# Pair steps of a stick-breaking attention layer: the scores of two units move from the even slots to the odd slots, between projection and values

## The chip, the cores and the metric

The kernel runs on one core of a Trainium2 chip. The metric is the device time of one execution, in microseconds. Before the change the median of three executions is 1330.95 us (1330.93 to 1331.21).

## What is computed

One decoder layer on 1024 tokens of width 1024, all in float32: RMS norm, an input projection, stick-breaking attention with 16 heads of 64 columns, cross-attention of 4 heads to 256 memory tokens, an output projection, and a SwiGLU block. The part that the change touches is the stick-breaking attention:

```
q, k, v, xq = split_cols(h @ w_in, [D_MODEL, D_MODEL, D_MODEL, X_WIDTH])
def block(args):                      # 128 queries of every head
    z = jnp.einsum('bhqd,bhkd->bhqk', qi, k).astype(jnp.float32) * SCALE
    past = kpos[None, :] < tpos[:, None]
    log_fail = jnp.where(past, jax.nn.log_sigmoid(-z), 0.0)
    after = lax.cumsum(log_fail, axis=3, reverse=True) - log_fail
    a = jnp.where(past, jnp.exp(jax.nn.log_sigmoid(z) + after), 0.0)
    return jnp.einsum('bhqk,bhkd->bhqd', a.astype(v.dtype), v)
```

The kernel takes sigmoid(-z) ("fail") and sigmoid(z) ("succ"), builds the running product of fail from right to left, and multiplies it with succ: that is the weight a.

## The kernel before

Five engines run five hand-written programs and meet through counting semaphores: TensorE (PE), VectorE (DVE), ScalarE (ACT), GpSimd (POOL) and the DMA queue of SyncE (SP). An engine works its program in the written order, so the order of the code is the order of the work.

**Precision.** Every matrix product with float32 operands is made of three matmuls: each operand is split into a high part (written by ACT, names with `_h`) and a low remainder (written by DVE, names with `_l`). A "chunk" below is the three matmuls of 512 columns that one block of 128 input rows adds to a projection.

**Pair steps.** The 16 heads are taken as 8 pairs. A pair step `s` (`pe_step`, `act_step`, `dve_step`) computes the attention of pair `s` and, woven into it, the q, k and v projections of pair `s + 1`: six parts of 512 tokens, eight chunks each (`pe_part`), which share one PSUM bank, `j_ps[:, 0]`. A part may begin only when ACT (`act_evac_half`, L494) and, for q and k, DVE (`dve_evac_half`, L601) have taken the previous part out of that bank. The steps 0 to 6 are of this kind (in a loop but for the outer ones); in the last step, 7, there is no next pair, and the first tiles of the output projection (`pe_project`, L1182) stand in the place of the parts.

**Units and slots.** The causal triangle of a pair is cut into ten units, 0 to 9 (`UNITS`), of 384 to 512 key columns for both heads. A step has ten slots. The work of unit `u` goes round the engines:

- PE makes its scores (`pe_scores`, L409) into one of two PSUM areas, `z2[u % 2]`, by parity of the unit. It waits for the second sigmoid of unit `u - 2`, which read the same area.
- ACT takes two sigmoids: `act_fail` (L506), which waits for the weights of unit `u - 2`, and `act_succ` (L512), which waits for the turns of unit `u - 2`.
- DVE scans fail for both heads (`dve_scan`, L617 and L622) and multiplies (`dve_weights`, L630).
- PE turns the weights, 6 or 8 transposes into `t_ps` (`pe_transposes`, L418), in slot `u`. It waits for the weights, and for the low part of the previous unit's turns, since `t_ps` is one buffer.
- ACT writes the high part of the turns, `a_h` (`act_high`, L521), DVE the low part, `a_l` (`dve_low`, L647).
- PE multiplies with v (`pe_values`, L436, 8 or 16 matmuls), after slots 1, 2, 3, 5, 7 and 9 (`VALUES_AT`). It waits for `a_l` of the last unit of its group and, in a group that opens a new bank content, for ACT's copies of the earlier result (`act_low_rows`, L533 and L534, four per group; `ROWS_AT` puts them in slots 2, 3 and 6).

After slot 9 `pe_v` (L391) turns the next pair's v; ACT and DVE take that out of `t_ps` too (L499, L606) before the turns of the next unit 0 may start. In slot `u` DVE's program has: scans of unit `u + 1` (with the low part of a projection half between the two heads, after `EVAC_LOW`), low part of unit `u`, weights of unit `u + 1`. The change leaves DVE's, POOL's and SP's programs as they are.

In an even slot PE has turns, then the scores of units `u + 2` and `u + 3`, then chunks, then perhaps values. In an odd slot it has turns, chunks, values. ACT has in each slot `u`: high part of `u`, copies of rows, fail and succ of unit `u + 2`, then a weight conversion (L487) or the high part of a finished projection half.

Of the kernel before, what the change touches and what calls it, by code (L numbers as in the profile page):

```python
# [19 lines left out]
def trunk(nc, x, mem, norms, w_mem_kv, w_out, w_gate, w_up, w_down, sb_w_in, out):  # L20
# [25 lines left out]
    NU = len(UNITS)  # L46
# [5 lines left out]
    ROWS_AT = {2: 0, 3: 2, 6: 5}  # L52
    SCANS_TO = (4, 6, 8, 12, 14, 16, 18, 20, 22, 24)
    CARRY_BY = {4: 4, 5: 4, 8: 7, 9: 8}
    PARTS = {1: (0, 5, 8), 2: (1, 0, 8), 3: (2, 0, 8), 4: (3, 0, 4), 5: (3, 4, 8), 6: (4, 0, 4), 7: (4, 4, 8),
             8: (5, 0, 4), 9: (5, 4, 8)}
    PART_END = {1: 0, 2: 1, 3: 2, 5: 3, 7: 4, 9: 5}
    EVAC_LOW = {2: 0, 3: 1, 4: 2, 6: 3}
    M0 = 2
# [28 lines left out]
    with ExitStack() as ctx:  # L88
# [354 lines left out]
        def pe_step(pe, s, par, last=False):  # L443
            for u in range(NU):
                if u:
                    pe_transposes(pe, s, u)
                if u == 0 and isinstance(s, int) and s == 0:
                    pe_scores(pe, s, 2, par)
                    pe_part(pe, s + 1, 1 - par, 0, 0, 2)
                    pe_scores(pe, s, 3, par)  # L450
                    pe_part(pe, s + 1, 1 - par, 0, 2, 3)
                    pe_transposes(pe, s, u)
                    pe_part(pe, s + 1, 1 - par, 0, 3, 5)
                    continue
                if u % 2 == 0:
                    for ahead in (u + 2, u + 3):
                        if ahead < NU:
                            pe_scores(pe, s, ahead, par)
                        elif not last:
                            pe_scores(pe, s + 1, ahead - NU, 1 - par)  # L460
                if not last and u == 0:
                    pe_part(pe, s + 1, 1 - par, 0, 0, 2)
                    pe_transposes(pe, s, u)
                    pe_part(pe, s + 1, 1 - par, 0, 2, 5)
                elif not last:
                    pe_part(pe, s + 1, 1 - par, *PARTS[u])
                else:
                    if u == 0:
                        for i, some in AHEAD:
                            pe_project(pe, i, some=some)  # L470
                        pe_transposes(pe, s, u)
                    for i, some in FILL.get(u, ()):
                        pe_project(pe, i, some=some)
                if u in VALUES_AT:
                    pe_values(pe, s, VALUES_AT[u], par)
            if not last:
                pe_v(pe, s + 1, 1 - par, 1 + TUSE * s + NU)
# [65 lines left out]
        def act_step(act, s, par, last=False):  # L543
            side = iter(SPLITS) if last else None
            for u in range(NU):
                if last and u - 1 in FILLED:
                    act_part(act, FILLED[u - 1])
                if u == 0:
                    act_fail(act, s, 2)
                    if last:  # L550
                        act_low_rows(act, s - 1, NU - 1, heads=(0,))
                act_high(act, s, u)
                if isinstance(s, int) and s == PAIRS - 2:
                    for i in PRE_AT.get(u, ()):
                        act_split(act, i)
                if last:
                    for _ in range(SPLIT_AHEAD[u]):
                        act_split(act, next(side))
                if u in ROWS_AT:
                    act_low_rows(act, s, ROWS_AT[u])  # L560
                nxt = (s, u + 2) if u + 2 < NU else (s + 1, u + 2 - NU) if not last else None
                if nxt:
                    if u:
                        act_fail(act, *nxt)
                    act_succ(act, *nxt)
                if last:
                    if u == 0:
                        act_low_rows(act, s - 1, NU - 1, heads=(1,))
                    for _ in range(SPLIT_RATE[u] - SPLIT_AHEAD[u]):
                        act_split(act, next(side))  # L570
                    continue
                for k in CONV_AT.get(u, ()):
                    if k < 6 or not (isinstance(s, int) and s == PAIRS - 2):
                        act_w(act, s + 1 + k // 6, k % 6, (1 - par + k // 6) % 2)
                if u in PART_END:
                    act.wait_ge(s_pj, W0 + 6 * (s + 1) + PART_END[u] + 1)
                    act_evac_half(act, s + 1, PART_END[u], 1 - par)
# [221 lines left out]
        for i in PRE + SPLITS + LATER + SECOND:  # L799
# [5 lines left out]
        SPLIT_AHEAD = (0, 0, 0, 0, 0, 0, 0, 0, 1, 1)  # L805
        DVE_RATE = (0, 0, 1, 1, 1, 1, 1, 2, 2, 2)
        DVE_AHEAD = (0,) * NU
        LOWER, UPPER = (0, 1), (2, 3, 4, 5)
        AHEAD = [(0, (0, 1))]
        FILL = {0: [(0, (2, 3, 4, 5))], 1: [(1, (0, 1, 2, 3))], 2: [(1, (4, 5))], 3: [(2, None)], 4: [(3, LOWER)],  # L810
                5: [(3, UPPER)], 6: [(4, None)], 7: [(5, None)], 8: [(6, None)], 9: [(7, None)]}
        FILLED = {0: 0, 2: 1, 3: 2, 5: 3, 6: 4, 7: 5, 8: 6, 9: 7}
        assert sum(SPLIT_RATE) == len(SPLITS) and sum(DVE_RATE) + sum(DVE_AHEAD) == sum(LOW[i][0] for i in SPLITS)
# [381 lines left out]
        def act_part(act, i):  # L1195
            act.wait_ge(s_op, i + 1)
            act.activation(part[:, i], out_bank(i), ACT.Copy).then_inc(s_pt, 1)
# [1063 lines left out]
        def _(pe):  # L2261
# [66 lines left out]
            for s in range(2):  # L2328
                pe_step(pe, s, s)
# [42 lines left out]
```

## Time and profile before

| | |
|---|---|
| median of three executions | 1330.95 us |
| the profiled execution | 1331.02 us |
| its span, first to last instruction | 1329.2 us |
| PE busy | 1314.0 us, 99% of the span |
| DVE busy | 1030.5 us, 78% |
| ACT busy | 680.7 us, 51% |
| POOL busy | 419.6 us, 32% |
| DMA queues, mean | 54 GB/s |
| granted TensorE clock | 1.0 in the whole span |

The profile page gives busy shares for the whole program; the stretch that the change touches is the part from 119 to 606 us, where the pair steps run. In the rows of the trace the first number is the start in us from the beginning of the span and the second the time from there to the end of the last instruction in the row. The matmuls overlap in the pipeline, so a matmul of 512 columns lasts 0.39 us in the records, while the next one starts 0.23 us after it. Start to start is the cost that counts.

### The profile page before, as it was taken

Reading aid. Unit: us, or ns where it says so; the run is one execution under the profiler, and the core shown is the slowest. Engines: PE = TensorE matmul, PEld = TensorE weight load, DVE = VectorE, ACT = ScalarE, POOL = GpSimd, SP = SyncE. Lnnn points to the kernel's source line nnn. Section 1 sums busy time; section 2 is a strip of 40 time slices with the busy share of each in tenths; the row PEclk is TensorE's granted clock in tenths of the full one; section 3 lists DMA queues with packets and bytes.
Section 4 is the critical chain, followed back from the end, with each engine's and each line's share of the span. In section 5 each row is a group of like instructions: output and inputs, shape, how many; then the busy total and the mean of one; then the engine's idle time right before and its main releaser. Section 6 shows DMA issues by size and latency. Waiting matters only on the chain.

```text
span 1329.2 us, 20179 instructions
## 1 busy us (share of the span) xinstructions
PE 1314.0 (99%) x6854; PEld 1088.7 (82%) x6854; DVE 1030.5 (78%) x1153; ACT 680.7 (51%) x1154; POOL 419.6 (32%) x307
## 2 busy tenths in 40 slices
PE   7999999999999999999999999999999999999999
PEld 5887888888888888888888788888888888888887
DVE  6577898887978899995258877878778787777866
ACT  7577676666666677773254433343343433333340
POOL 2000000000000001214034764747546484664721
PEclk9999999999999999999999999999999999999999
DMA  7100100010010101206111222121212112122103
GB/s 254 32 25 24 33 25 25 25 33 25 24 32 24 32 24 40 104 9 199 31 40 32 73 74 61 40 72 32 71 47 63 61 36 69 39 71 62 42 32 127
DMA packets 91484, 71.87 MB, mean 54 GB/s; under 512 B 4256, under 2 KB 75936, under 8 KB 91424
## 3 DMA queue, kind: packets, MB, share of 16 engines
q1 hardware_dynamic: 91424, 71.07, 17.0%
q8 instruction: 37, 0.61, 0.2%
q14 instruction: 23, 0.19, 0.0%
HBM read 65.03 MB, written 4.19 MB: 52 GB/s over the span
## 4 chain that ended last, share of the span: by engine, by line
PE 93%; DVE 2%; ACT 2%; POOL 1%; issue 1%; DMA 0%; ACTq 0%; POOLq 0%; DVEq 0%
PE ps L1476 27%; PE ps L378 16%; PE ps L1651 14%; PE ps L1182 8%; PE ps L436 5%; PE ps L418 5%; PE ps L409 4%; PE ps L1261 3%; PE ps L344 3%; PE ps L1706 2%; PE ps L958 1%; PE ps L898 1%; ACT junk L839 1%; PE ps L1069 1%; PE ps L1134 1%
## 5 line engine op out<-in xcount | busy, mean ns | idle before, releaser
L1661 DVE TENSOR_TENSOR x<-ps,x 128x2048 f32<-128x2048 f32 x70 | 160.3, 2290 | 92.6 <-PE ps L1651 92.6
L655 POOL TENSOR_TENSOR o_t<-o_t,pv_low 128x256 f32 x24 | 21.4, 890 | 445.1 <-ACT o_t L534 445.1
L1444 DVE TENSOR_TENSOR part_l<-part_x,part_h 128x512 fp32r<-128x512 f32 x140 | 141.7, 1036 | 25.3 <-POOL part_x L1422 17.9
L1639 POOL TENSOR_TENSOR bl<-bx_B,bh 128x512 fp32r<-128x512 f32 x70 | 93.2, 1331 | 208.8 <-ACT bh L1635 208.8
L378 PE MATMUL ps<-hh,w_h 128*128 128x512 f32 x336 | 139.1, 414 | 0.0
L521 ACT ACTIVATE a_h<-ps 128x1024 fp32r<-128x1024 f32 (+1 forms) x80 | 75.4, 942 | 116.0 <-PE ps L418 115.7
L378 PE MATMUL ps<-hh,w_l 128*128 128x512 f32 x336 | 131.6, 392 | 0.0
L378 PE MATMUL ps<-hl,w_h 128*128 128x512 f32 x336 | 131.0, 390 | 0.0
L1476 PE MATMUL ps<-ft_h,part_h 128*128 128x512 f32 x320 | 124.5, 389 | 0.0
L1476 PE MATMUL ps<-ft_l,part_h 128*128 128x512 f32 x320 | 124.5, 389 | 0.0
L1476 PE MATMUL ps<-ft_h,part_l 128*128 128x512 f32 x320 | 124.5, 389 | 0.0
L1487 ACT ACTIVATE kept<-ps 128x512 f32<-128x512 f32 x60 | 35.7, 595 | 158.2 <-PE ps L1476 158.2
L1651 PE MATMUL ps<-bh,ah 128*128 128x512 f32 x280 | 109.1, 390 | 0.9 <-DVE x L1661 0.6
L1651 PE MATMUL ps<-bl,ah 128*128 128x512 f32 x280 | 108.9, 389 | 0.0
L617 DVE TENSOR_TENSOR_SCAN fail<-fail,own 128x257 f32<-128x257 f32 (+3 forms) x128 | 101.1, 828 | 9.4 <-ACT fail L506 9.4
L647 DVE TENSOR_TENSOR a_l<-ps,a_h 128x1024 fp32r<-128x1024 f32 (+1 forms) x80 | 89.0, 1113 | 22.5 <-ACT a_h L521 22.2
L1635 ACT ACTIVATE bh<-bx_B 128x512 fp32r<-128x512 f32 x70 | 44.2, 631 | 102.5 <-PE ps L1651 97.9
L1476 PE MATMUL ps<-f_h,part_h 128*128 128x512 f32 x240 | 93.4, 389 | 0.0
L1476 PE MATMUL ps<-f_l,part_h 128*128 128x512 f32 x240 | 93.4, 389 | 0.0
L1476 PE MATMUL ps<-f_h,part_l 128*128 128x512 f32 x240 | 93.4, 389 | 0.0
L1437 ACT ACTIVATE part_h<-part_x 128x512 fp32r<-128x512 f32 x140 | 82.9, 621 | 19.6 <-POOL part_x L1411 14.7
L630 DVE TENSOR_TENSOR succ<-fail,succ 128x1024 f32<-128x1024 f32 (+2 forms) x80 | 91.0, 1137 | 0.7
(290 smaller groups left out, 3390.6 us busy)
## 6 DMA issues: line engine op xcount, KB each, us to landing
w_raw<-in_sb_w_in SPq DMA_DIRECT2D x52, 256.0 KB, 2.8
bx_B<-in_w_down SPq DMA_DIRECT2D x44, 256.0 KB, 3.0
part_x<-in_w_gate SPq DMA_DIRECT2D x40, 256.0 KB, 2.9
part_x<-in_w_up SPq DMA_DIRECT2D x40, 256.0 KB, 2.8
wo_raw<-in_w_out SPq DMA_DIRECT2D x20, 256.0 KB, 3.3
x_in<-in_x SPq DMA_DIRECT2D x8, 512.0 KB, 7.5
x<-in_x SPq DMA_DIRECT2D x16, 256.0 KB, 5.4
out<-x SPq DMA_DIRECT2D x16, 256.0 KB, 2.0
```

The costliest lines, as they stand in the source:

```text
L378: mm = pe.matmul(j_ps[:, 0], w[:, kc // 4, kc % 4], h[:, kc, half * BANK:(half + 1) * BANK], start=(kc == 0 and i == 0), stop=(kc == KC - ...
L521: act.activation(home(a_h), t_ps[:, :, 0:len(blocks_of(u)) * P].rearrange("p h (j q) -> p h j q", q=P), ACT.Copy).then_inc(s_th, 1)
L617: dve.tensor_tensor_scan(back, back, own[:, BANK - w:BANK + 1][:, ::-1], 0.0, ALU.mult, ALU.max).then_inc(s_scan, 1)
L630: done = dve.tensor_tensor(g, f[:, :, 1:w + 1], g, ALU.mult)
L647: dve.tensor_tensor(home(a_l), t_ps[:, :, 0:len(blocks_of(u)) * P].rearrange("p h (j q) -> p h j q", q=P), home(a_h).bitcast(F32), ALU.sub ...
L1182: mm = pe.matmul(out_bank(i), o[:, t % 4 * P:t % 4 * P + P], w[k][:, :], start=(at_ == 0 and j == 0), stop=(at_ == len(order) - 1 and j == 2))
L1437: act.activation(part_h[p][:, :, :].rearrange(flat), part_x[m][p][:, :, :].rearrange(flat), ACT.Copy).then_inc(s_fh, 1)
L1444: dve.tensor_tensor(part_l[m][p][:, :, :].rearrange(flat), part_x[m][p][:, :, :].rearrange(flat), part_h[p][:, :, :].rearrange(flat).bitca ...
L1476: mm = pe.matmul(product_bank(m, p), w[:, k], g[:, k], start=(p in (0, 1, 3) and k == 0 and i == 0), stop=(k == 3 and i == 2), skip_group_ ...
L1639: pool.tensor_tensor(bl[(par + k) % 2][:, :], bx[B_OPS[k]][:, :], bh[(par + k) % 2][:, :].bitcast(F32), ALU.subtract).then_inc(s_bw, 1)
L1651: mm = pe.matmul(ps[:, t], g[:, t * P:(t + 1) * P], w[:, :], start=(k in (0, 4, 5) and i == 0), stop=(i == 2), skip_group_check=True)
L1661: dve.tensor_tensor(o, ps[:, 0:4], o, ALU.add).then_inc(s_x2, 1)
```

## The change

PE: the scores of two units leave the even slots. They now stand in the odd slots, behind the chunks and in front of the values, and are those of units `u + 3` and `u + 4`. The chunks are split anew: slots 4, 6 and 8 have six chunks each and slots 5, 7 and 9 two (before, four in each); slot 0 has seven chunks of the first part and slot 1 one (before, five and three). The last step's output projection is divided in the same manner (`LOWER`, `UPPER`, `AHEAD`, `FILL`).

ACT: in the odd slots fail and succ of unit `u + 2` go ahead of the high part of unit `u`. In the even slots the order stays.

```diff
-    PARTS = {1: (0, 5, 8), 2: (1, 0, 8), 3: (2, 0, 8), 4: (3, 0, 4), 5: (3, 4, 8), 6: (4, 0, 4), 7: (4, 4, 8),
-             8: (5, 0, 4), 9: (5, 4, 8)}
+    PARTS = {1: (0, 7, 8), 2: (1, 0, 8), 3: (2, 0, 8), 4: (3, 0, 6), 5: (3, 6, 8), 6: (4, 0, 6), 7: (4, 6, 8),
+             8: (5, 0, 6), 9: (5, 6, 8)}
...
                     pe_transposes(pe, s, u)
-                    pe_part(pe, s + 1, 1 - par, 0, 3, 5)
-                    continue
-                if u % 2 == 0:
-                    for ahead in (u + 2, u + 3):
-                        if ahead < NU:
-                            pe_scores(pe, s, ahead, par)
-                        elif not last:
-                            pe_scores(pe, s + 1, ahead - NU, 1 - par)
-                if not last and u == 0:
-                    pe_part(pe, s + 1, 1 - par, 0, 0, 2)
+                    pe_part(pe, s + 1, 1 - par, 0, 3, 7)
+                elif not last and u == 0:
+                    pe_part(pe, s + 1, 1 - par, 0, 0, 4)
                     pe_transposes(pe, s, u)
-                    pe_part(pe, s + 1, 1 - par, 0, 2, 5)
+                    pe_part(pe, s + 1, 1 - par, 0, 4, 7)
...
+                if u % 2:
+                    for ahead in (u + 3, u + 4):
+                        if ahead < NU:
+                            pe_scores(pe, s, ahead, par)
+                        elif not last:
+                            pe_scores(pe, s + 1, ahead - NU, 1 - par)
                 if u in VALUES_AT:
                     pe_values(pe, s, VALUES_AT[u], par)
...
+                nxt = (s, u + 2) if u + 2 < NU else (s + 1, u + 2 - NU) if not last else None
+                if nxt and u % 2:
+                    act_fail(act, *nxt)
+                    act_succ(act, *nxt)
                 act_high(act, s, u)
...
-                nxt = (s, u + 2) if u + 2 < NU else (s + 1, u + 2 - NU) if not last else None
-                if nxt:
+                if nxt and u % 2 == 0:
                     if u:
                         act_fail(act, *nxt)
                     act_succ(act, *nxt)
...
-        LOWER, UPPER = (0, 1), (2, 3, 4, 5)
-        AHEAD = [(0, (0, 1))]
-        FILL = {0: [(0, (2, 3, 4, 5))], 1: [(1, (0, 1, 2, 3))], 2: [(1, (4, 5))], 3: [(2, None)], 4: [(3, LOWER)],
+        LOWER, UPPER = (0, 1, 2, 3), (4, 5)
+        AHEAD = [(0, (0, 1, 2))]
+        FILL = {0: [(0, (3, 4, 5))], 1: [(1, (0, 1, 2, 3))], 2: [(1, (4, 5))], 3: [(2, None)], 4: [(3, LOWER)],
```

PE's program at the boundary of slots 5 and 6 of an ordinary step, before: values of slot 5, turns of unit 6, scores of units 8 and 9, then the first of four chunks (the numbers behind names only tell buffers apart).

```order
L378 MATMUL ps<-hh,w_l_77 128x512
L436 MATMUL ps<-a_h,v_s_71 128x256
...
L418 MATMUL ps<-ident,succ 128x128 x6
L409 MATMUL ps<-k_h_69,q_h_67 128x512 x2
L409 MATMUL ps<-k_l_70,q_h_67 128x512 x2
L409 MATMUL ps<-k_h_69,q_l_68 128x512 x2
...
L378 MATMUL ps<-hh,w_h_74 128x512
```

The same place now:

```order
L378 MATMUL ps<-hh,w_l_77 128x512
L409 MATMUL ps<-k_h_69,q_h_67 128x512 x2
L409 MATMUL ps<-k_l_70,q_h_67 128x512 x2
L409 MATMUL ps<-k_h_69,q_l_68 128x512 x2
...
L436 MATMUL ps<-a_h,v_s_71 128x256
...
L418 MATMUL ps<-ident,succ 128x128 x6
L378 MATMUL ps<-hh,w_h_74 128x512
```

The scores have gone from behind the turns of unit 6 to ahead of the values of slot 5, and the chunks of slot 6 stand right behind the turns.

ACT's program in slot 5 of an ordinary step, before: the high part of unit 5's turns, then fail and succ of unit 7, then the high part of a finished half of k (the register rows only compute semaphore targets).

```order
L521 ACTIVATE a_h<-ps 128x8x128
L503 REGISTER_ALU
L506 ACTIVATE fail<-ps 128x2x512
L512 ACTIVATE succ<-ps 128x1024
L576 REGISTER_ALU
L494 ACTIVATE k_h_65<-ps 128x512
```

And now:

```order
L505 ACTIVATE fail<-ps 128x2x512
L510 REGISTER_ALU
L511 ACTIVATE succ<-ps 128x1024
L520 ACTIVATE a_h<-ps 128x8x128
L578 REGISTER_ALU
L493 ACTIVATE k_h_65<-ps 128x512
```

Both sigmoids have moved ahead of the high part. The same holds in slots 1, 3, 7 and 9.

## Rows read from the trace of the kernel before

**Rows 1.** Windows, an ordinary step: length, then PE, PEld, DVE, ACT, POOL busy

```profile
243.76:303.72 59.96, 59.96 (x379) 50.55 (x378) 51.33 (x60) 39.92 (x59) 3.57 (x4) 1.00 0.09 27
```

**Rows 2.** Timeline of PE, slots 7 and 8 of that step

```profile
287.49 1.03 PE L418 MATMUL ps<-ident,succ 128*128 128x128 f32 x8
288.28 0.48 PE L378 MATMUL ps<-hh,w_h 128*128 128x512 f32 x1
288.60 0.40 PE L378 MATMUL ps<-hl,w_h 128*128 128x512 f32 x1
...
291.10 0.28 PE L436 MATMUL ps<-a_h,v_s 128*128 128x256 f32 x1
...
292.93 1.06 PE L418 MATMUL ps<-ident,succ 128*128 128x128 f32 x8
293.92 0.33 PE L409 MATMUL ps<-k_h,q_h 64*128 64x128 f32 x2
...
295.33 0.50 PE L378 MATMUL ps<-hh,w_h 128*128 128x512 f32 x1
```

**Rows 3.** Timeline of ACT and DVE, slot 7

```profile
288.56 1.03 ACT L521 ACTIVATE a_h<-ps 128x1024 fp32r<-128x1024 f32 x1 [0.95 <-PE ps L418]
289.49 1.02 ACT L506 ACTIVATE fail<-ps 128x1024 f32<-128x1024 f32 x1
290.39 1.03 ACT L512 ACTIVATE succ<-ps 128x1024 f32<-128x1024 f32 x1
...
289.62 1.22 DVE L647 TENSOR_TENSOR a_l<-ps,a_h 128x1024 fp32r<-128x1024 f32 x1 [0.43 <-ACT a_h L521]
290.77 1.22 DVE L630 TENSOR_TENSOR succ<-fail,succ 128x1024 f32<-128x1024 f32 x1
```

**Rows 4.** Timeline, slot 6: turns on PE, both sigmoids on ACT

```profile
282.29 0.82 PE L418 MATMUL ps<-ident,succ 128*128 128x128 f32 x6
...
285.67 1.03 ACT L506 ACTIVATE fail<-ps 128x1024 f32<-128x1024 f32 x1
286.60 1.02 ACT L512 ACTIVATE succ<-ps 128x1024 f32<-128x1024 f32 x1
```

**Rows 5.** The chain that ended last: scores of units 8 and 9

```profile
283.10 1.59 PE ps L409 x12
```

**Rows 6.** Timeline of PE, step 0: scores behind a chunk

```profile
124.37 0.39 PE L378 MATMUL ps<-hh,w_l 128*128 128x512 f32 x1
124.69 0.33 PE L409 MATMUL ps<-k_h,q_h 64*128 64x128 f32 x2
```

**Rows 7.** Timeline of PE: values that had waited for DVE, step 6

```profile
542.34 0.39 PE L436 MATMUL ps<-a_h,v_s 128*128 128x256 f32 x1
```

**Rows 8.** Timeline, from the turns of v to unit 1

```profile
243.76 1.03 PE L391 MATMUL ps<-ident,v_t 128*128 128x128 f32 x8
...
249.70 0.93 DVE L647 TENSOR_TENSOR a_l<-ps,a_h 128x768 fp32r<-128x768 f32 x1
...
250.32 0.39 PE L378 MATMUL ps<-hh,w_l 128*128 128x512 f32 x1
250.69 0.88 PE L418 MATMUL ps<-ident,succ 128*128 128x128 f32 x6
```

**Rows 9.** Timeline of DVE, slots 1 and 2

```profile
253.40 0.95 DVE L647 TENSOR_TENSOR a_l<-ps,a_h 128x768 fp32r<-128x768 f32 x1
...
255.19 0.67 DVE L601 TENSOR_TENSOR q_l<-ps,q_h 128x512 fp32r<-128x512 f32 x1
```

**Rows 10.** Timeline of the last step: PE and ACT, slots 2 and 5

```profile
556.48 1.06 PE L418 MATMUL ps<-ident,succ 128*128 128x128 f32 x8
...
559.84 0.38 ACT L534 ACTIVATE om_t<-ps 64x256 f32<-64x256 f32 x1
...
572.98 1.09 PE L418 MATMUL ps<-ident,succ 128*128 128x128 f32 x8 [0.51 <-DVE succ L630]
```

## The prediction, made before the changed kernel ran

> **What bounds the kernel now.** I read the page first: PE is busy in 99% of the span at a granted clock of 1.0. The windows view of one ordinary pair step says the same of the stretch that the change touches: PE's records fill 59.96 of 59.96 us, DVE's 51.33, ACT's 39.92 [rows 1]. So a step lasts as long as PE's instructions take, start to start, and there is nothing to win from a wait that goes away, since hardly one is left. The change can shorten a step only where it makes PE's changes of work cheaper, and lengthen it wherever PE comes to a wait before the other engines are ready. So I read the timelines of PE, ACT and DVE for how long before its need each hand-over is ready.
>
> In slot 7 PE starts the turns at 287.49, the chunks 0.79 later, and the values at 291.10, 3.61 after the turns [rows 2]. The values need unit 7's low part. ACT starts the high part 1.07 after the turns' start, DVE the low part 1.06 after that, and it ends at 290.84, 3.35 after the turns [rows 3]. From the end of a DVE instruction to the start of PE's that waited for it are 0.06 us (249.70 + 0.93 to 250.69) [rows 8]. So the values are free to start at 3.41 and do at 3.61: the reserve is 0.2 us. This round (turns, high part, low part, values) is what the change lengthens.
>
> **The change, part by part.** The amounts are the same: no matmul, sigmoid, scan or DMA is added or removed. All is in the order.
>
> *Changes of work on PE.* Scores use 64 rows of the array for each head, all else 128. Before, a batch of scores stands between turns and chunks: turns to scores cost 0.99 instead of the 0.79 of turns to chunks (0.20), the batch of units 0 and 1 takes 1.41 up to the first chunk, whose record is 0.50 instead of 0.48 (0.02) [rows 2]. Together 1.63. Now it stands between chunks and values. From a chunk's last matmul to scores are 0.32 instead of 0.23 (0.09) [rows 6]. How scores are followed by values the trace does not show. Below, the values' first matmul costs nothing more; above, the 0.11 by which a first values matmul that had waited is longer (0.39 against 0.28) [rows 7, 2]. That gives 1.50 to 1.61 for a batch, so 0.02 to 0.13 saved, five batches a step. I take 0.06, near the upper price, since the first chunk behind scores pays too: 0.3 us a step.
>
> The Trainium skill, "TensorEngine Tiling (Array Packing)", section "Key Properties", says that a change of tiling mode drains TensorE. By that rule alone the saving would be nothing, since each batch has one change in and one out before as well as after, and the step's sum would be 0.3 higher; the rows above show that the two ways in are not priced alike (0.20 and 0.09).
>
> *ACT's order in odd slots, slot 7.* fail of unit `u + 2` can run early: it waits only for the weights of unit `u`, which are ready when the turns start. succ must wait until the turns have read its buffer, so it starts where the high part started, 1.07 after the turns' start. It takes 0.90 (from fail to succ, 289.49 to 290.39) [rows 3]. ACT works in order, so the high part starts at 1.97, the low part at 3.03, ends at 4.25, and the values may start at 4.31. PE has now two chunks there: 0.79, then six matmuls (0.32 for the first, 0.227 for each other by the eleven from 288.60 to 291.10, 1.46), 0.09, scores 1.41: it arrives at 3.75 [rows 2, 6]. That alone is a wait of 0.56.
>
> In slot 7 ACT is late besides. Slot 6 has the four copies of rows; its fail of unit 8 starts 3.38 and its succ 4.31 after the turns of unit 6 [rows 4]. Then fail of unit 9 comes at 5.22 and succ at 6.13. PE has in slot 6 now six turns (0.59, two fewer than 0.79 at 0.10 each) and 18 matmuls (4.18), so the turns of unit 7 start at 4.77, and succ could have gone at 5.84. So everything is 0.29 later: the values wait 0.85.
>
> *Slots 5 and 9.* The same sum. In slot 5 the scores are those of units 8 and 9, 1.59 [rows 5]: PE arrives at 3.93, the wait is 0.38. In slot 9 succ is of 384 columns a head, an estimate of 0.70 from the 0.90 for 512, so the values are free at 4.11; the scores of units 2 and 3 lie between 1.41 and 1.59: 0.18 to 0.36, I take 0.25. In slots 1 and 3 the longer round is hidden: slot 1's values are of unit 0, and in slot 3 eight chunks stand ahead.
>
> *Slot 0.* The turns of unit 1 start 6.93 after the turns of v, when DVE has unit 0's low part [rows 8]. That side (v out, copies of rows, fail and scan of unit 2, low part) stays. PE arrives before at 250.55, so it waits 0.14. Now it has no scores there but seven chunks: 0.79 + 12 matmuls 2.82 + turns 0.59 + 9 matmuls 2.14 = 6.34. Wait 0.59, 0.45 more.
>
> *Slot 2.* The part that starts here needs DVE's low part of the q half before it, which ended 5.17 after the turns of unit 1 (255.86 − 250.69) [rows 8, 9]; DVE's side of it stays. Scores used to stand between turns and that part. Now PE has, from the turns of unit 1: 0.59, one chunk 0.87 (its end to scores included), scores at most 1.59, eight values 0.92 (half of the 1.83 for sixteen) [rows 2] plus 0.11, turns 0.79: 4.87. Ready at 5.23. Wait 0.36. In slot 6 the like wait (low part of k) comes out at nothing or 0.1.
>
> *An ordinary step:* 0.85 + 0.38 + 0.25 + 0.45 + 0.36 = 2.29, less 0.3: about +2.0. DVE and POOL have no instruction moved, and the stretch after the steps is PE's own work, so nothing gives this back. I take steps 0 to 6 as seven such steps: +14.0.
>
> *The last step.* Slot 2 has only six projection matmuls. Its values wait for the copies of rows, which end 3.74 after the turns of unit 2 (560.22 − 556.48) [rows 10]; the scores (1.6) covered that. Now PE arrives at 0.79 + 1.46 = 2.25: wait 1.55. In slot 4, PE waits 0.51 for the weights of unit 5 already [rows 10]; it has six more matmuls (1.37) for the scores that left (1.63): 0.26 more. Slot 5 adds 0.38. Together +2.2; an unpriced one is output tile 4, which comes sooner behind the turns of unit 6 and needs DVE's last split.
>
> **Sum:** 14.0 + 2.2 = 16.2 us on the profiled 1331.02 (its span of 1329.2 and 1.8 around it; 0.07 above the median): 1347.
>
> **The rivals.**
>
> *Only the value waits count,* 1341. The waits of slots 0 and 2 are differences of long sums on both sides, and a small shift of DVE's work could clear them. Left: 0.85 + 0.38 + 0.25 − 0.3 = 1.2, times seven, and about 2 for the last step: +10. Against it: slot 0 had a wait even before. Chance 15%.
>
> *Faster:* PE's cheaper entry into scores counts and no wait shows. Place: the values of slots 5, 7 and 9. It holds if the low part comes before PE: the round would have to be 0.56 shorter than 4.31 in slot 7, for instance if succ did not hold up the high part. Then 40 batches at 0.02 to 0.13 save 1 to 5 us: 1328. For it: PE's share is full now, and every wait that I found is below 1 us. Against it: the round is made of four measured pieces in strict order, its reserve before was 0.2, and the change adds 0.90. Chance 8%.
>
> *No change,* both sides cancel: 1331. Chance 3%.
>
> *The lateness runs on:* 1354. ACT's lateness after slot 6 or DVE's in slots 6 to 8 adds waits at turns too, and the last step's split costs 1 or more: 3 us a step. For it: DVE has 51 of 60 us of work, and low part, weights and scan follow each other. Against it: in even slots six chunks (4.97 with the turns) stand against a round of 4.56 (high part, low part and weights start 1.07, 1.06 and 1.15 apart, the weights take 1.22, and 0.06 [rows 3, 8]). Chance 8%.
>
> *The forecast:* 66%.
>
> **Numbers.** 1347 us. Its own bounds: waits of slots 9 and 2 and the saving at their ends, 1.6 to 2.4 a step, 1343 to 1351. With the first rival below and part of the last above, the range is 1338 to 1352. A measurement of this kernel tells about 0.2% (2.7 us) from no change. Slower by more than that: 66 + 15 + 8 = 89%; within: 3%; faster: 8%.
>
> **What would show it.** An ordinary step (from turns of v to turns of v) should be 62 us for 59.96. PE should have waits named for DVE's low part ahead of the values of slots 5, 7 and 9, near 0.4, 0.85 and 0.25; ahead of the turns of unit 1, 0.6; ahead of the first chunk of slot 2, 0.36, for DVE's q_l; and in the last step one of 1.5 for ACT's copies. The high part in slot 7 should start some 2.2 after the turns. I am wrong if values start with no gap behind scores, or if scores to values cost much more than 0.11: at 0.3 the two values that don't wait (slots 1 and 3) would add 0.4 a step.

## The result, and the profile after

The changed kernel takes 1353.27 us (median of five executions, 1351.8 to 1355.2) against 1330.95 (five executions, 1330.73 to 1331.22); the ratio is 1.0169, 95% interval 1.0158 to 1.018. It is 22.3 us slower. The forecast was 1347, range 1338 to 1352: the sign was right, the time 1.3 us above the range.

The windows view of the changed kernel, the eight pair steps from one turn of v to the next. Columns: stretch, its length, busy us of PE, PEld, DVE, ACT, POOL, then granted clock, DMA share, GB/s.

```profile
120.40:185.88 65.48, 63.39 (x403) 51.95 (x402) 55.52 (x66) 41.38 (x59) 2.78 (x3) 1.00 0.09 25
185.88:247.94 62.06, 60.31 (x378) 50.05 (x377) 51.90 (x60) 39.92 (x59) 3.57 (x4) 1.00 0.09 27
247.94:310.05 62.11, 60.43 (x379) 50.03 (x378) 51.91 (x60) 39.92 (x59) 3.54 (x4) 1.00 0.09 26
310.05:372.14 62.09, 60.41 (x378) 50.03 (x377) 51.81 (x60) 39.92 (x59) 3.55 (x4) 1.00 0.09 27
372.14:438.01 65.87, 62.16 (x378) 51.21 (x377) 51.94 (x60) 39.92 (x59) 3.55 (x4) 0.97 0.09 25
438.01:500.14 62.13, 60.47 (x378) 50.03 (x377) 51.80 (x60) 39.93 (x59) 3.56 (x4) 1.00 0.09 26
500.14:562.80 62.66, 60.68 (x378) 49.98 (x377) 56.77 (x65) 45.64 (x70) 10.65 (x8) 1.00 0.13 40
562.80:626.58 63.78, 58.69 (x343) 47.56 (x342) 52.34 (x57) 41.05 (x63) 7.47 (x7) 1.00 0.18 61
```

The third row answers to [rows 1]: the step has become 2.15 us longer, while PE's busy time is up only by 0.47 and DVE's by 0.58. PE waits now. Before, the same eight stretches were 63.34, 60.03, 59.96, 59.91, 59.95, 59.92, 60.85 and 59.99. The differences are 2.14, 2.03, 2.15, 2.18, 5.92, 2.21, 1.81 and 3.79, together 22.23. That is the whole loss: PE's long run of output projection behind the steps (255 matmuls in the chain, 57.84 us both times) begins at 626.58 for 604.34. So there are three things to explain: a toll of about 2.1 in each of seven steps (14.7), an event of 3.7 in step 4 alone, and the last step's 3.8.

Step 0 and the last step are not like the others in the amount of work. The same view of the kernel before, step 0 and the last step:

```profile
120.10:183.44 63.34, 61.19 (x386) 50.87 (x385) 55.12 (x66) 41.36 (x60) 2.79 (x3) 1.00 0.09 26
544.34:604.33 59.99, 59.43 (x361) 49.45 (x360) 52.05 (x57) 41.43 (x64) 7.21 (x7) 1.00 0.18 63
```

Step 0 still makes the scores of units 2 and 3 at its head and now makes five more batches, one more than before (PE x403 for x386). The last step has one fewer (x343 for x361), since step 6 makes that of its units 2 and 3. A batch is about 1.6 us. So the last step is 3.8 longer with 1.6 less to do, and 1.6 of what step 0 has added is work; it is only 2.14 longer because PE had waited there for the low part twice before, 1.08 and 1.06 in the records.

PE's waits in the changed kernel: who waited for whom, us in total, times, the longest.

```profile
PE ps L436 <- DVE a_l L649: 7.4, 15, 0.7
...
PE ps L418 <- DVE a_l L649: 2.9, 7, 0.5
PE ps L378 <- issue: 2.9, 2, 2.4
...
PE ps L436 <- ACT om_t L533: 1.4, 1, 1.4
PE ps L418 <- DVE v_s L608: 1.4, 1, 1.4
PE ps L1184 <- DVE o_l L999: 0.8, 1, 0.8
PE ps L418 <- DVE succ L632: 0.7, 1, 0.7
...
PE ps L378 <- DVE q_l L603: 0.4, 1, 0.4
```

The reader should see that the page's share (PE 98% busy) hides them: in the steps each is under a microsecond but for three, and the list counts only what is left after the modelled end of the matmul before. Start to start is more exact, and for that I laid the step's PE records side by side. The timeline of the changed kernel in slot 7, all three engines (it answers to [rows 2, 3]):

```profile
292.43 1.03 PE L418 MATMUL ps<-ident,succ 128*128 128x128 f32 x8
292.72 1.03 ACT L505 ACTIVATE fail<-ps 128x1024 f32<-128x1024 f32 x1
...
293.62 1.05 ACT L511 ACTIVATE succ<-ps 128x1024 f32<-128x1024 f32 x1
...
294.53 1.05 ACT L520 ACTIVATE a_h<-ps 128x1024 fp32r<-128x1024 f32 x1
295.62 1.22 DVE L649 TENSOR_TENSOR a_l<-ps,a_h 128x1024 fp32r<-128x1024 f32 x1 [1.20 <-ACT a_h L520]
...
296.97 0.38 PE L436 MATMUL ps<-a_h,v_s 128*128 128x256 f32 x1 [0.72 <-DVE a_l L649]
```

The high part starts 2.10 after the turns (before: 1.07), the low part ends 4.41 after them, and the values start at 4.54 for 3.61.

Step 2 of both kernels in pieces, each from its first start to the first start of the next piece, in us (worked out from PE's timelines; for scores that stood in another slot before, the slot is named):

| piece | before | after | added by waiting |
|---|---|---|---|
| slot 0, the nine matmuls ahead of the turns of unit 1 | 2.30 | 2.71 | 0.41 |
| slot 2, turns to first chunk (where none waits: 0.80) | | 1.16 | 0.36, for q_l |
| slot 5, scores of units 8 and 9 (before in slot 6) | 1.60 | 1.99 | 0.39 |
| slot 7, scores of units 0 and 1 (before in slot 8) | 1.41 | 2.20 | 0.79 |
| slot 9, scores of units 2 and 3 (before in slot 0) | 1.59 | 1.78 | 0.19 |
| sum | | | 2.14 |
| all turns, q_l's wait left out | 8.91 | 8.11 | |
| all chunks, the wait of slot 0 left out | 34.16 | 34.54 | |
| all values | 9.30 | 9.72 | |

The last three rows are the price of the changes of work: 0.80 less, 0.38 more, 0.42 more. The batches cost the same in either place.

Then the event of step 4, which no row of before has. PE's timeline of the changed kernel where step 4 begins:

```profile
372.14 1.03 PE L391 MATMUL ps<-ident,v_t 128*128 128x128 f32 x8
375.60 0.49 PE L378 MATMUL ps<-hh,w_h 128*128 128x512 f32 x1 [2.42 <-issue]
375.93 0.39 PE L378 MATMUL ps<-hl,w_h 128*128 128x512 f32 x1
376.16 0.40 PE L378 MATMUL ps<-hh,w_l 128*128 128x512 f32 x1
376.39 0.60 PE L378 MATMUL ps<-hh,w_h 128*128 128x512 f32 x1
376.79 0.63 PE L378 MATMUL ps<-hl,w_h 128*128 128x512 f32 x1
...
379.77 0.42 PE L378 MATMUL ps<-hh,w_l 128*128 128x512 f32 x1
380.03 0.81 PE L418 MATMUL ps<-ident,succ 128*128 128x128 f32 x6
```

After the turns of v PE does nothing for 2.4 us, and the releaser is "issue": no semaphore held it. Then come three matmuls at the usual pace and eight at 0.40 to 0.43 start to start for 0.23, about half pace. The windows view of those 3.64 us of the changed kernel (the clock is the number ahead of the DMA share):

```profile
376.39:380.03 3.64, 3.64 (x10) 2.78 (x9) 1.23 (x1) 0.51 (x1) 0.38 (x1) 0.53 0.14 42
```

The granted clock is 0.53 here for 1.00 in the ordinary steps: nearly all of this stretch at the lower of the clock's two levels, 1.2 GHz, and ahead of it PE had stood still. The place is where PE's loop over steps 2 to 5 (two steps a turn) branches back to its start. The page's part on DMA queues says how much code was fetched. Before, it was 37 packets of instructions; now:

```profile
q8 instruction: 46, 0.75, 0.2%
```

Nine packets more, of 16 KB each by the row. The DMA view of a stretch alone says when. The changed kernel, 371.9 to 499, which is the second turn of the loop (steps 4 and 5):

```profile
q8 instruction: 8, 0.13, 0.5%
```

In the kernel before the same view from 353 to 483.5 has no packet of instructions at all: its loop ran its second turn on code that was already there. In the changed kernel that code was fetched again. (The ninth packet starts at 371.29, just ahead of the event.)

The last step, the four longest of PE's waits (timeline of the changed kernel, rows apart):

```profile
567.28 0.85 PE L418 MATMUL ps<-ident,succ 128*128 128x128 f32 x6 [1.36 <-DVE v_s L608]
...
580.80 0.36 PE L436 MATMUL ps<-a_h,v_s 128*128 128x256 f32 x1 [1.43 <-ACT om_t L533]
...
595.03 1.09 PE L418 MATMUL ps<-ident,succ 128*128 128x128 f32 x8 [0.72 <-DVE succ L632]
...
606.49 0.50 PE L1184 MATMUL ps<-wo_h,o_h 128*128 128x512 f32 x1 [0.83 <-DVE o_l L999]
```

### The profile page after: what moved, and what is told of

Its sections match the earlier page's. It is cut to its first block, busy times and chain, and to the rows that moved or that the text cites. A ratio compares the mean times of both kernels' runs of the same rounds, so it can differ in the third digit from the quotient of the medians.

```text
span 1351.5 us, 20169 instructions
## 1 busy us (share of the span) xinstructions
PE 1320.2 (98%) x6854; PEld 1086.1 (80%) x6854; DVE 1034.5 (77%) x1153; ACT 680.7 (50%) x1154; POOL 419.7 (31%) x307
## 4 chain that ended last, share of the span: by engine, by line
PE 80%; DVE 6%; ACT 6%; issue 5%; POOL 1%; DMA 0%; ACTq 0%; DVEq 0%; SPq 0%; POOLq 0%
PE ps L1478 27%; PE ps L1653 14%; PE ps L378 11%; PE ps L1184 7%; PE ps L436 5%; PE ps L418 3%; PE ps L1263 3%; PE ps L344 3%; DVE a_l L649 2%; ACT a_h L520 2%; DVE fail L619 2%; PE ps L1708 2%; PE ps L409 1%; ACT fail L505 1%; DVE succ L632 1%
## 5 line engine op out<-in xcount | busy, mean ns | idle before, releaser
L1439 ACT ACTIVATE part_h<-part_x 128x512 fp32r<-128x512 f32 x140 | 83.0, 621 | 19.6 <-POOL part_x L1413 14.7
```

The lines of the kernel that those rows point to most:

```text
L1439: act.activation(part_h[p][:, :, :].rearrange(flat), part_x[m][p][:, :, :].rearrange(flat), ACT.Copy).then_inc(s_fh, 1)
```

## The experiments

### The event: is it the order of the work, or the loop?

**The changed kernel with PE's loop written out.**

```diff
-            with pe.Fori(1, LOOPS) as m:
+            for m in range(1, LOOPS):
```

> The changed kernel with PE's loop over the middle pair steps written out (steps 2 to 5 in line, no branch back); the other engines keep their loops, and the order of the work is the same. In the changed kernel the fifth step lasts 65.87 us and its neighbours 62.1: PE stands 2.42 us for nothing but issue right where its loop has branched back, and then ten matmuls run at half the clock. Theory A (code loading): the loop's code is fetched again when it branches back, so in line there is no such stall: all middle steps 62.1, no fall of the clock, about 3.8 us less than the changed kernel, 1349.5. Rival B (the stall comes with the new order of the work): it stays, 1353. The Trainium skill, Advanced Engine Details and Errata, section ISA Cache, gives TensorE's instruction cache as 128 KB in lines of 16 KB; that is for theory A, and it says nothing on how lines are thrown out.

Measured: 1349.61 us (1349.53 to 1349.73), ratio 1.0140 (1.0123 to 1.0157). Step 4 is 62.08, the half pace is gone, and there are 43 packets. The event is gone with the branch back: 3.7 us. Writing the loop out moves the code too, so this alone doesn't prove that the branch is to blame. The place of the stall does the rest: in each of the four profiles that have it, PE stops right behind the branch back.

**The kernel before, with 72 waits on a semaphore long reached (36 instructions) ahead of the pair steps.**

```diff
+            for _ in range(72):
+                pe.wait_ge(s_id, 1)
```

> The kernel before with 36 more instructions ahead of PE's first matmul (waits that are met while PE is idle anyway), so that its loop over the middle steps starts where the changed kernel's does. Theory A (code loading, decided by where the loop lies in the code): the fifth step gets the stall after the branch back and the half clock, 59.9 to about 63.7, 1334.8 in all, and the instruction queue moves some 46 packets instead of 37. Rival B (the stall comes with the new order): nothing changes, 1331.0, 37 packets. Between them: the loop is refetched but PE's work ahead hides it.

Measured: 1335.01 us (1334.68 to 1335.68), ratio 1.0031 (1.0019 to 1.0044). The order of the work is that of before, but the stall is there in step 4 (63.14 for 59.95), with 46 packets again. That is 3.2 of the 3.7 us by which the span of the profiled execution is longer; the rest was not traced. PE's timeline of this run:

```profile
363.77 1.03 PE L391 MATMUL ps<-ident,v_t 128*128 128x128 f32 x8
367.21 0.50 PE L409 MATMUL ps<-k_h,q_h 64*128 64x512 f32 x2 [2.41 <-issue]
...
370.57 0.50 PE L378 MATMUL ps<-hl,w_h 128*128 128x512 f32 x1 [0.59 <-issue]
```

All six executions lie above 1334. So the stall does not need the moved scores: 36 instructions ahead of the loop are enough. The half pace isn't part of it each time: here none follows.

**The kernel before with its loop written out**, the control (the same edit as the first).

> Control: the kernel before with PE's loop over steps 2 to 5 written out. Theory A: it had no reload (37 instruction packets, no step longer than 60.0 among 1 to 5), so nothing changes but the number of packets, 43: 1331 within 0.5. Rival B: the loop's branch costs the kernel before something too: 1329 or less.

Measured: 1331.87 us (1331.8 to 1331.92, ten executions), ratio 1.0006 (0.9996 to 1.0016), steps of 60.03. Writing the loop out wins nothing where there is no stall; the time is even 0.8 us longer than the 1331.07 measured beside it.

**The changed kernel, 160 such waits (80 instructions), and with 320 (160 instructions).**

> The changed kernel with 80 more instructions that do nothing (waits on a semaphore already reached) in PE's program ahead of the pair steps. Theory A: whether PE's loop is fetched again when it branches back depends on where its start and end lie against the 16 KB packets in which code comes in. The end moves further into its last packet, the start stays in the same one: the stall stays, 46 instruction packets or more, time near 1353 to 1354. Rival B: the stall is chance or hangs on an exact instant: then it comes and goes, 1349.5 or 1353.

> As the run before, with 160 more instructions in place of 80. Theory A: the start of the loop now lies in the next packet, and the loop spans one packet fewer, as in the kernel before: no stall of 2.4 us and no half clock after it, all ordinary steps 62.1, 38 or 39 instruction packets in all, time 1349.5 to 1350. Rival B: any shift keeps it: 1353.

Measured: 1354.15 us (1353.72 to 1354.6) and 1363.05 us (1362.65 to 1363.55). The totals mislead, because the waits themselves were not free this time: step 0 begins at 124.28 and 133.96 for 120.40 (in the run with 36 they were hidden). By the steps, both are without the event. The nearer one's step 4 in the windows view:

```profile
376.00:438.10 62.10, 60.44 (x378) 50.04 (x377) 51.81 (x60) 39.89 (x59) 3.57 (x4) 1.00 0.09 25
```

Both have 38 packets. Less their 3.9 and 13.6 us they stand at 1350.3 and 1349.5. For the far one theory A was right but for the cost of the waits; for the near one it was wrong: I expected the stall to stay. That code ahead of the loop can take the event away as well as bring it is borne out (the four executions of each run lie within 0.9 us); my rule for which places are bad is not.

### The ordinary step: which part of the change costs what?

**The kernel before with ACT's new order alone** (sigmoids ahead of the high part in odd slots; PE's program is that of before).

```diff
+                nxt = (s, u + 2) if u + 2 < NU else (s + 1, u + 2 - NU) if not last else None
+                if nxt and u % 2:
+                    act_fail(act, *nxt)
+                    act_succ(act, *nxt)
                 act_high(act, s, u)
...
-                if nxt:
+                if nxt and u % 2 == 0:
```

> The kernel before with one part of the change alone: in odd slots ACT takes fail and succ of unit u + 2 ahead of the high part of unit u; PE's order is the old one. Theory: the values of slots 5, 7 and 9 are free at 4.31 (4.11 in slot 9) after the turns, and PE with four chunks comes at 3.61: waits of 0.7, 0.7 and 0.5, and slot 6's rows make ACT late in slot 7, up to 0.3 more. A middle step 59.9 + 2.0 = 61.9, 1331 + 7 x 2.0 + 0.7 in the last step = 1346. Rival: ACT's order costs little alone, and it is the scores in the odd slots that make the waits: below 1335.

Measured: 1348.68 us (1348.54 to 1348.79), ratio 1.0133 (1.0116 to 1.015), 2.7 above what I expected; ordinary steps 62.17 to 62.26. Its waits in one such step are three, all ahead of values. The group of values' matmuls with a_h in step 3 (count, busy and mean, then idle time before and its releaser):

```profile
L436 PE MATMUL ps<-a_h,v_s 128*128 128x256 f32 (+1 forms) x41 | 10.1, 283 | 1.5 <-DVE a_l L650 1.5
```

Start to start they are 0.73, 0.80 and 0.51 in slots 5, 7 and 9, and each run of values behind such a wait takes 0.1 more (1.93 for 1.83 in slot 7), which I had left out; the last step became 1.9 longer for my 0.7. ACT's part of the change alone costs 2.3 us a step, more than the whole change (2.15). PE's new order hides a part of that by putting the scores into the gap, and pays for it in slots 0 and 2.

**The changed kernel with the high part between fail and succ.**

```diff
                 if nxt and u % 2:
                     act_fail(act, *nxt)
+                act_high(act, s, u)
+                if nxt and u % 2:
                     act_succ(act, *nxt)
-                act_high(act, s, u)
```

> The changed kernel, with ACT's odd slots in the order fail, high part, succ, instead of fail, succ, high part. Theory of the prediction (the 0.90 of succ in the round turns, high part, low part, values makes PE wait in slots 5, 7 and 9): the high part starts 1.07 after the turns, the values are free at 3.41 and PE comes at 3.75 to 3.93, so the three waits (0.37, 0.72 and 0.22 measured) go, and the scores of the second unit, which need succ, are free at 3.05 and are reached at 3.1: a middle step 62.1 - 1.3 = 60.8, over 7 steps 9 us and 0.4 in the last step, about 1344 with the stall after the branch back, 1340 without. Rival: PE then waits for succ ahead of the second batch of scores instead, and the step stays at 62. Slots 0 and 2 (0.45 and 0.36) should be as they are in the changed kernel under either.

Measured: 1341.18 us (1341.11 to 1344.52), ratio 1.0085 (1.0068 to 1.0102); steps of 60.93 to 60.98. In the ordinary steps no value waits for the low part any more. What is left of the excess (0.97 in the step that begins at 245.75) are the turns of unit 1, as in the changed kernel, and scores that wait for the second sigmoid, which is now last on ACT: units 4 and 5 take 1.90 for 1.58, units 0 and 1 take 1.72 for 1.41. The turns of unit 2 to the first chunk are back to 0.84 too, without a change in DVE's order: the scores of units 4 and 5, which come 0.3 later, cover q_l's wait. From this profile, slot 7 (PE is held some 0.2 before the scores of unit 1, until succ ends at 293.01):

```profile
291.05 1.05 ACT L520 ACTIVATE a_h<-ps 128x1024 fp32r<-128x1024 f32 x1
291.95 1.06 ACT L511 ACTIVATE succ<-ps 128x1024 f32<-128x1024 f32 x1
...
292.75 0.28 PE L409 MATMUL ps<-k_h,q_l 64*128 64x256 f32 x2
293.06 0.45 PE L409 MATMUL ps<-k_h,q_h 64*128 64x384 f32 x2
...
293.79 0.39 PE L436 MATMUL ps<-a_h,v_s 128*128 128x256 f32 x1
```

PE's program in this run is the changed kernel's, instruction for instruction, and yet its profile has 37 packets and no stall; one execution of the four took 3.3 us more, at a mean clock of 0.997. So the place of PE's code isn't all that decides about the event.

**The changed kernel with ACT's old order** (high part, fail, succ).

> The changed kernel, but ACT keeps its old order in the odd slots too (high part, then fail and succ). Theory A: the low part is there at 3.4 after the turns, so no value waits for DVE, but the second unit's scores in the odd slots need succ of unit u + 2, which now ends near 3.9 after the turns where PE arrives near 3.05: waits of 0.5 to 1.2 inside the scores of slots 1, 5, 7 and 9 and the old 0.4 of slot 0, so an ordinary step of 63 to 64.5 and a time of 1353 to 1365. Rival B: the sigmoids ahead of the high part are the whole loss, and without them the step is near 60.6 and the time near 1336.

Measured: 1363.3 us (1362.54 to 1364.39), ratio 1.0243 (1.0226 to 1.026), ordinary steps of 63.7. PE's waits, first row:

```profile
PE ps L409 <- ACT succ L511: 17.3, 29, 0.8
```

The values wait no longer, the scores do, 29 times: 2.64 for 1.58 in slot 1, 2.54 for 1.60 in slot 5, 2.34 for 1.41 in slot 7, 2.10 for 1.59 in slot 9, together 3.4 us a step. With scores in the odd slots, ACT's sigmoids are wanted early and its high part as well, and it can do only one of them first. Theory A was right, at the upper end of its range; rival B, that the sigmoids' place was the whole loss, falls. Part of the time is the event, which this profile has as well: step 4 is 67.7, with 46 packets. PE's timeline of this run, and the windows view from there:

```profile
381.52 0.79 PE L378 MATMUL ps<-hh,w_h 128*128 128x512 f32 x1 [2.73 <-issue]
```

```profile
381.52:384.93 3.41, 3.41 (x9) 2.70 (x10) 1.23 (x1) 0.99 (x1) 0.73 (x1) 0.53 0.02 5
```

**The changed kernel with 160 idle waits (80 instructions, 1354.15), and DVE taking q's low part in slot 2 ahead of its first scan.**

```diff
+                if u == 2 and not last:
+                    dve_evac_half(dve, s + 1, EVAC_LOW[u], 1 - par)
                 if nxt and u > 1:
                     dve_scan(dve, *nxt, 0)
-                if u in EVAC_LOW and not last:
+                if u in EVAC_LOW and u != 2 and not last:
...
```

> The changed kernel with the 80 idle instructions that took its reload away (1354.15 us), and in slot 2 DVE takes the low part of the finished q half ahead of its first scan and not behind it. Theory A: the 0.36 us by which the first chunk of slot 2 starts late is the wait for this low part, which stood behind a scan of 1.0 us; q's high part is there 0.9 us earlier. Then the turns of unit 2 to the first chunk take 0.80 for 1.16, a step 61.75 for 62.10, and the time is 1351.6. Rival B: DVE's scan comes later by 0.6, the weights behind it too, and the wait only moves to the turns of unit 3 or to the values: 1354.

Measured: 1352.0 us (1351.96 to 1352.31), ratio 1.0158 (1.0141 to 1.0175); steps 61.73 for 62.10. The timeline of this run in slot 2:

```profile
262.05 0.68 DVE L603 TENSOR_TENSOR q_l<-ps,q_h 128x512 fp32r<-128x512 f32 x1
262.53 1.06 PE L418 MATMUL ps<-ident,succ 128*128 128x128 f32 x8
...
263.34 0.48 PE L378 MATMUL ps<-hh,w_h 128*128 128x512 f32 x1
```

Turns to chunk are 0.81 for 1.16, and nothing else in the step got later: it is 0.37 shorter, the whole of the wait.

### The last step

**The changed kernel, the last step in the order of before** (scores in even slots, high part first, the old division of the output projection; step 6 then issues no scores in slot 9).

```diff
                 else:
+                    if u % 2 == 0:
+                        for ahead in (u + 2, u + 3):
+                            if ahead < NU:
+                                pe_scores(pe, s, ahead, par)
...
-                if u % 2:
+                if u % 2 and not last and not (u == NU - 1 and isinstance(s, int) and s == PAIRS - 2):
...
-                if nxt and u % 2:
+                if nxt and u % 2 and not last:
...
-        LOWER, UPPER = (0, 1, 2, 3), (4, 5)
+        LOWER, UPPER = (0, 1), (2, 3, 4, 5)
...
```

> The changed kernel, but the last step (7) keeps the order of before: scores behind the turns of even slots, high part ahead of the sigmoids, two chunks of the output projection ahead; step 6 therefore issues no scores in slot 9. Theory A: the last step's excess (3.8 us: 63.78 against 59.99) comes from the scores that left slots 0, 2 and 4 and had covered DVE's v_s (wait 1.36), ACT's copies of rows (1.43) and a split of o_l (0.83). With them back the last step lasts 60.0 to 60.5, the waits named go, step 6 is 0.2 to 0.6 shorter, and the time is about 1349.5. Rival B: the last step is late because DVE and POOL come late out of step 6 with the splits, whatever PE's order: then it stays over 62 and the time over 1351.5.

Measured: 1348.14 us (1345.78 to 1349.99), ratio 1.013 (1.0113 to 1.0147). The windows of this run, steps 6 and 7:

```profile
498.06:560.77 62.71, 59.09 (x360) 48.63 (x359) 56.75 (x65) 45.61 (x70) 10.65 (x8) 1.00 0.13 40
560.77:621.17 60.40, 59.53 (x361) 49.38 (x360) 52.47 (x57) 41.30 (x63) 8.31 (x7) 1.00 0.19 65
```

The last step is 60.40 for 63.78, and of its waits 0.3 for v_s and 0.5 for the weights of unit 5 are left; the latter stood there before too [rows 10]. So the lateness was one of cover: DVE and POOL are no less busy than in the changed kernel (52.47 and 8.31 for 52.34 and 7.47). Step 6 did not get shorter, as I had expected: without scores in slot 9 its values wait 1.68 for the low part. The event is in this profile (a stall of 2.28) without the half pace: step 4 is 64.13. The four executions of this one kernel are 1345.78, 1347.87, 1348.42 and 1349.99. The lowest is 2.1 under the profiled one, which is what the stall cost in it (64.13 for 62.08), and the highest is 2.1 above. I read this as one execution without the event and one with the half pace; only the one of 1347.87 was profiled, so it is argued from the times.

**All repairs together:** the last step of this run, the high part between the sigmoids, q's low part first.

> All repairs together: the scores stay in the odd slots of steps 0 to 6, but ACT takes the high part between fail and succ, DVE takes q's low part ahead of the scan in slot 2, and the last step has its old order. Theory A: the ordinary step is that of the run with the high part between, 60.95, since what is left of its excess is the turns of unit 1 (0.4) and two scores that wait for succ (0.3 each); the last step falls from 63.6 to 60.4: 1341.2 - 3.2 = 1338.0. Still slower than before, since the batches cost PE the same in either place, so that nothing is won by moving them. Rival B: the place between chunks and values is cheaper, as the forecast had it (0.3 a step): then under 1336.

Measured: 1337.28 us (1337.26 to 1342.28), ratio 1.0059 (1.004 to 1.0079). Its windows, step 3 and the last:

```profile
306.06:366.94 60.88, 60.39 (x378) 49.86 (x377) 51.43 (x60) 39.92 (x59) 3.76 (x4) 1.00 0.09 27
550.06:610.56 60.50, 59.52 (x361) 49.42 (x360) 52.59 (x57) 41.28 (x63) 8.41 (x7) 1.00 0.19 65
```

The time is 0.7 under the forecast of theory A and still 6.2 above the 1331.07 measured beside it. One of the four executions took 5.0 more than the others; the profiled one has 37 packets and no event. The new place wins nothing to set against the waits that remain. No run here is under 1331.

## Why the prediction was wrong in its time, and where it was right

**The waits of the ordinary step: right.** Forecast 0.38, 0.85, 0.25, 0.45 and 0.36 for slots 5, 7, 9, 0 and 2; measured 0.39, 0.79, 0.19, 0.41 and 0.36. The values start at 4.33, 4.54 and 4.11 after their turns for the forecast 4.31, 4.60 and 4.11. The largest, slot 7's, was 0.06 smaller: the high part came 2.10 after the turns, not 2.26. The timeline explains the 0.06: PE's turns of unit 7 came 4.93 after those of unit 6 for the forecast 4.77, so ACT was 0.16 less late, but the low part started 1.09 behind the high part for 1.06, and the values 0.13 behind its end for 0.06. Two of the causes were shown by removing them: the sigmoids ahead of the high part (slots 5, 7 and 9; 60.95 for 62.1) and the scan ahead of q_l (slot 2; 61.73 for 62.10). The term of slot 0 rests on the timeline alone. The ordinary step became 2.15 longer for the forecast 2.0, and the seven steps together 14.7 for 14.0. Some of this closeness is luck. Two errors run against each other: the waits were 2.14 for 2.29, and the 0.3 that I took off was not there. And step 0 is no ordinary step: its 2.14 hold a batch of 1.6 more, less two waits that it had before.

**The changes of work: mis-sized.** I took 0.3 us a step for cheaper entries into scores; the pieces sum to 0.00. What the turns saved (about 0.20 four times, since turns pass to chunks more cheaply than to scores) went to the chunks, which now pass into scores (1.54 to 1.55 for six), and to the first values behind scores. The rule of the Trainium skill, "TensorEngine Tiling (Array Packing)", section "Key Properties", that each change of tiling mode drains TensorE, gave nothing saved. This trace agrees in the sum (0.00 over five batches), though the single entries are not priced alike.

**The last step: the term was too small**, 2.2 for a measured 3.8. The three waits that I had priced came out: from the first projection matmul of slot 2 to its first values are 3.06 for 1.51, which is the forecast 1.55; slot 4 costs 0.22 more for 0.26, and slot 5's values 0.38 for 0.38. What I had left out is on both sides. The first turns wait for DVE's v_s, 1.36 in the records, where the scores that left slot 0 had been the cover; but those scores, 1.6 us, are themselves no longer in this step, so that the two about cancel. What remains are output tile 4's wait for its split, 0.83 in the records and 1.08 start to start, which I named and did not price, and some 0.4 before the turns of unit 1 (0.25 of it a recorded wait for a_l). That all of these come from the order of the last step was shown (60.40 with the old order); the share of each was read, not tried apart.

**A term was absent: 3.7 us for the branch back of PE's loop.** This is the step that failed: the forecast added seven ordinary steps and the last one and put nothing for a turn of the loop. Without the event the time would have been 1349.6, as with the loop written out, inside the range. The rival "the lateness runs on", 1354, gave nearly the measured time by another mechanism, which is refuted: it asked for 3 us a step.

**What stays open:** what decides about the event. The Trainium skill, "Advanced Engine Details and Errata", section "ISA Cache", says that TensorE's instruction cache holds 128 KB in lines of 16 KB, 256 instructions. The row on packets agrees with the line (0.75 MB in 46), and the eight packets of the second turn are 128 KB. The same section says "Only 2 cache lines!"; the kernel before, which fetched six packets in the loop's first turn (243.5 to 363.6) and none in its second, doesn't agree. What is kept at a branch the section does not say. That 36 instructions bring the stall, 80 more take it from the changed kernel, and the same code for PE has it or not with another order on ACT, no rule of mine explains.

The traces have one more sign. In the four profiles with the event, one packet of instructions starts 0.85 to 1.01 us before step 4's turns of v and takes 0.93 to 1.35: it lands between 0.08 us before and 0.49 us after the start of those turns, behind which the loop branches back (in the changed kernel it starts at 371.29, the turns at 372.14). In the seven profiles that keep the loop and lack the event, the last packet starts 4.8 to 17.3 us before those turns, and none follows until the loop is done. With the high part between the sigmoids, whose code for PE is the changed kernel's, that packet does not come at all before the branch. This fits a race between the fetch of the code behind the loop and the branch back, which a few instructions or a small shift in time can tip; it would also explain why executions of one kernel differ, as those with the old last step do. The changed kernel's own five go from 1351.8 at a mean clock of 1.0 to 1355.2 at 0.997. It is a reading of eleven profiles, not tried by an experiment.

## What to carry to other kernels

Before moving work out of a gap, ask for each wait around the old place what covered it: the scores that moved had covered waits for v_s, for ACT's copies and for a split in the last step, and those of slots 0 and 2 in the ordinary one. Count the batches of the first and the last step apart: they need not have what the others have. An engine that serves two rounds in one slot (here ACT: the sigmoids for the next scores, the high part for the next values) can't be reordered at no cost; either order was tried, and one in between lost least. And when a step inside a loop differs from its neighbours, look for a stall released by "issue" and for the instruction packets in that stretch before looking for a reason in the order of work.

## What was unexpected of the hardware

A loop that PE had run once cost a stall of 2.3 to 2.7 us at its branch back in some kernels and nothing in others, with 46 instruction packets for 37; 36 instructions that do nothing, ahead of it, were enough to bring it on (1335.01 for 1330.96). In two profiles the pause was followed by a stretch at a granted clock of 0.53, most of it at the lower level of 1.2 GHz: 3.6 us behind a stall of 2.42 in the changed kernel, 3.4 us behind one of 2.73 with ACT's old order. In two others (stalls of 2.41 and 2.28) PE stood about as long and the clock stayed at 1.00. And 160 waits on a semaphore already reached took PE 3.9 us of the kernel's time, 320 took 13.6, while 72 were hidden: even filler for shifting code has to be measured.
